# The norms of the two mixers: one full-precision product over all 512 squares, and a factor by logarithm and exponential

## The chip, the core and the metric

The kernel runs on one core of a Trainium2 chip. The metric is the device time of one execution in microseconds; below 1% of that time is a few of them, so small sums matter here. A core has TensorE (PE, with its weight loads shown apart as PEld), VectorE (DVE), ScalarE (ACT), GpSimd (POOL) and SyncE (SP), which issues nearly all DMAs. Each engine runs its own list of instructions in order and waits on semaphores.

## The reference, cut to what matters

One decoder block over 2048 tokens of 1024 features: an input projection, two mixers side by side (a gated linear recurrence with 4 heads of 128, and sliding-window attention with 8 heads of 64), an output projection over both, and a SwiGLU feed-forward network.

```python
# gated recurrence: each head is normed by itself, over its 128 features
o = o.transpose(0, 2, 3, 1, 4).reshape(bsz, s, A_HEADS, A_DV)
o = o * lax.rsqrt(jnp.mean(o * o, axis=-1, keepdims=True) + EPS)
o = o.reshape(bsz, s, A_WIDTH) * norm_g.astype(f32) * jax.nn.silu(g.astype(f32))
...
# attention: normed over all 512 features of its 8 heads
o = o.reshape(bsz, s, B_WIDTH)
return rmsnorm(o, norm_g).astype(q.dtype)
...
h = h + jnp.concatenate([y_a, y_b], axis=-1) @ w_out[l]
```

So per token there are five factors 1/sqrt(mean of squares + EPS): one for each of the four recurrence heads, one for the attention. They are what the change computes in another way.

## The kernel before, in words

The mixers run over four blocks of 512 tokens (`it` = 0 to 3). Features lie on the 128 partitions, the 512 tokens along the free dimension, so the sum of squares over features runs across partitions and is made by TensorE. Dense products split each operand in two parts of reduced precision, `hi` and `lo`, and run three products (lines 831 to 833); `whi`/`wlo`, `uhi`/`ulo` and `yhi`/`ylo` are such pairs. What is not split runs in full float32.

The order of all work is written out by hand. A block has slots 0 to 26. In slots 0 to 21 TensorE makes one group of 128 input columns (24 products of 512 tokens, `group`), and then the small steps of the mixers. In slots 22 to 26 it makes the first half of the output projection instead (`out_a`, by pieces k: 22 has k = 0 and 1; 23 has 2; 24 has 4 and 5; 25 has 6; 26 has 7 and 3), then `out_b` makes the other half. Piece k below 4 needs recurrence head k finished (`ylo`, L1809), piece k from 4 the attention's pair k - 4. Head a begins in slot 4, 9, 14 and 18; each later step has an offset from it. Every engine walks the same slots with its own code, and an instruction that waits holds up all that is behind it on its engine.

The norm of head a, in before:

- NORM_SUM, offset 6 (slots 10, 15, 20, 24). ScalarE has squared the head's output into `sqo`. TensorE runs `sums` (L847): four products with a 128x128 square block as weights and one column of `ones` moving, into bank X[3]. ScalarE takes the square root of 4 columns (L1264) into `hnrm`, VectorE the reciprocal (L1799) into `hrnrm`.
- NORM_MUL, offset 7 (slots 11, 16, 21, 25). TensorE runs `spread` (L838): four products of the factor's column, broadcast as weights, with the identity; this lays the factor of each token on all partitions of X[3]. VectorE multiplies `gate` by X[3] (L1805), ScalarE and VectorE split the result into `yhi` (L1268) and `ylo` (L1809).

The attention's norm does the same once a block, on bank X[1]: sum in slot 21 (root L1394, reciprocal L1861), spread in slot 22, then four multiplications (L1814), one for each pair.

Other names that the steps use: `make_hi` (L1201) and `make_lo` (L1663) split the weights of the unit two slots ahead, and can begin only when TensorE is through with the unit that lies in that buffer, that is with this slot's group; `cuminv` (L1752, VectorE) feeds `key` (L2243, GpSimd), which the product L970 of the next slot needs; `x_turn` number j (L1024; one a slot from slot 19 on) transposes a piece of x into X[0], and waits until ScalarE has copied number j - 1 out (`h`, L1307); `stats` (L1208, two in slot 24) and `roots` (L1214) prepare the norm of the next block's x, and VectorE scales that x after them (L1671, L1676). ScalarE holds one set of function tables at a time, and ACT_TABLE_LOAD changes it; Copy and Square need no change.

Of the kernel before, what the change touches and what calls it, by code (L numbers as in the profile page):

```python
# [36 lines left out]
ALU = mybir.AluOpType  # L37
ACT = mybir.ActivationFunctionType
AX_X = mybir.AxisListType.X

P = 128
# [89 lines left out]
def block_program(nc, x, ln1_g, w_in, lb_logits, hgrn_norm_g, attn_sinks, attn_norm_g, w_out, ln2_g,  # L131
# [37 lines left out]
    with ExitStack() as ctx:  # L169
# [80 lines left out]
        nrm = sb("nrm", [P, TB]); rnrm = sb("rnrm", [P, TB])  # L250
        hnrm = sb("hnrm", [P, TB]); hrnrm = sb("hrnrm", [P, TB])
        snrm = sb("snrm", [P, TB]); srnrm = sb("srnrm", [P, TB])
        mx = sb("mx", [P, 2]); nm = sb("nm", [P, 2, 2]); nms = sb("nms", [P, 2])
# [159 lines left out]
        s_srr = sem("s_srr")  # L413
        s_smul = sem("s_smul")
        s_yb = sem("s_yb")
# [31 lines left out]
        s_arr = sem("s_arr")  # L447
        s_amul = sem("s_amul")
        s_ya = sem("s_ya")
# [376 lines left out]
        def _(pe):  # L826
# [17 lines left out]
            def sums(bank, squares, done):  # L844

                for b in range(TB):
                    last = mm(bank[:, b:b + 1], squares[:, b * P:(b + 1) * P], ones[:, 0:1], start=True, stop=True)  # L847
                last.then_inc(done, 1)

# [102 lines left out]
            def iv_turn(it, a):  # L952
                pe.wait_ge(s_iv, it * HEADS + a + 1)
                if a:
                    pe.wait_ge(s_ya, it * HEADS + a)
                elif it:
                    pe.wait_ge(s_osb, it * TB)
                for b in range(TB):
                    last = tr(X[3][:, b * P:(b + 1) * P], ivT[:, b * P:(b + 1) * P], ident[:, :])
                last.then_inc(s_ivtr, 1)  # L960
# [49 lines left out]

            def head_mul(it, a):
                pe.wait_ge(s_arr, it * HEADS + a + 1)
                spread(X[3], hrnrm, s_amul)

# [33 lines left out]
            def slots(it):  # L1048

                for slot in range(SLOTS):  # L1050
                    if slot < IN_GROUPS and (it or slot >= 2):
                        group(it, slot)
                    for k in A_PLAN.get(slot, ()):
# [3 lines left out]
                        if k == A_PLAN[OUT_A][0]:  # L1057
                            key_turn(it, HEADS - 1)
                    a = head_at(slot, NORM_MUL)
                    if a is not None:  # L1060
                        head_mul(it, a)
                    a = head_at(slot, UPDATE)
# [4 lines left out]
                    if slot == SWA_SUM:  # L1067
                        pe.wait_ge(s_oacc, it * (PAIRS - 1) + PAIRS - 1)
                        sums(X[1], sqs[0], s_ssum)
                    if slot == SWA_MUL:  # L1070
                        pe.wait_ge(s_srr, it + 1)
                        spread(X[1], srnrm, s_smul)
                    for begin, step in ((SCORE, scores), (P_TURN, p_turn), (PV, pv)):
# [16 lines left out]
            def out_b(it):  # L1090
                for c, bank in zip(range(4, CS), (1, 2, 3, 0)):
                    n = OUT_B + c - 4
                    if bank == 1:
                        pe.wait_ge(s_yb, it * PAIRS + PAIRS)

# [96 lines left out]
        def _(act):  # L1192
# [61 lines left out]
            def output(it, a):  # L1254
                act.wait_ge(s_o, it * HEADS + a + 1)
                if a:
                    act.wait_ge(s_asum, it * HEADS + a)
                A(sqo[:, :], X[2][:, :], ACT.Square).then_inc(s_sq, 1)

            def head_sum(it, a):  # L1260
                act.wait_ge(s_asum, it * HEADS + a + 1)
                if a:
                    act.wait_ge(s_arr, it * HEADS + a)
                A(hnrm[:, :], X[3][:, 0:TB], ACT.Sqrt, scale=1.0 / P, bias=epst[:, 0:1]).then_inc(s_aroot, 1)  # L1264

# [87 lines left out]
            def slots(it):  # L1353
                for slot in range(SLOTS):
# [37 lines left out]
                    if slot == SWA_SUM:  # L1392
                        act.wait_ge(s_ssum, it + 1)
                        A(snrm[:, :], X[1][:, 0:TB], ACT.Sqrt, scale=1.0 / (PAIRS * P),  # L1394
                          bias=epst[:, 0:1]).then_inc(s_sroot, 1)
                    if slot == SWA_MUL:
# [237 lines left out]
        def _(dve):  # L1634
# [158 lines left out]

            def head_sum(it, a):
                n = it * HEADS + a
                dve.wait_ge(s_aroot, n + 1)
                if a:
                    dve.wait_ge(s_amul, n)
                V.reciprocal(hrnrm[:, :], hnrm[:, :]).then_inc(s_arr, 1)  # L1799

            def head_mul(it, a):
                n = it * HEADS + a
                dve.wait_ge(s_amul, n + 1)
                dve.wait_ge(s_y1, n + 1)
                V.tensor_tensor(gate[a % 2][:, :], gate[a % 2][:, :], X[3][:, :], ALU.mult).then_inc(s_ya, 1)  # L1805

# [5 lines left out]
            def swa_mul(it, p):  # L1812
                dve.wait_ge(s_osq, it * PAIRS + p + 1)
                V.scalar_tensor_tensor(out=oT[p][:, :], in0=oT[p][:, :], scalar=gb[:, p:p + 1],  # L1814
                                       in1=X[1][:, :], op0=ALU.mult, op1=ALU.mult).then_inc(s_yb, 1)

# [6 lines left out]
            def slots(it):  # L1823
                for slot in range(SLOTS):
# [32 lines left out]
                    if mul is not None:  # L1857
                        head_lo(it, mul)
                    if slot == SWA_SUM:
                        dve.wait_ge(s_sroot, it + 1)  # L1860
                        V.reciprocal(srnrm[:, :], snrm[:, :]).then_inc(s_srr, 1)  # L1861
                    if slot == SWA_MUL:
                        dve.wait_ge(s_smul, it + 1)
                        swa_mul(it, 0)
                    i = step_at(slot, PV)
                    if i is not None and i % TB == TB - 1:
                        dve.wait_ge(s_pv, it * STEPS + i + 1)
                        V.tensor_copy(oT[i // TB][:, :], M[3][:, :]).then_inc(s_oT, 1)
                    for offset, step in ((KEYS, keys), (UPDATE, update), (OUTPUT, output), (NORM_SUM, head_sum)):
                        a = head_at(slot, offset)  # L1870
# [472 lines left out]
```

## Time and profile before

| | us |
|---|---|
| before, median of 3 runs | 2281.8 |
| before, the 3 runs | 2279.1, 2281.8, 2285.85 |
| the profiled execution, its own time | 2285.81 |
| its span, first to last instruction | 2284.0 |
| TensorE busy in it | 2222.6 (97%) |
| VectorE busy | 1438.3 (63%) |
| ScalarE busy | 1010.2 (44%) |
| GpSimd busy | 443.8 (19%) |
| mean granted clock of TensorE | 0.992 |

The span is nearly the whole time. The four mixer blocks end about 958 us into the span, and the rest is the feed-forward network, which the change does not touch. TensorE's busy share is an upper figure, since its products are pipelined. The profile's chain of work that ended last is 86% TensorE.

### The profile page before, as it was taken

The page shows a single profiled execution, that of the slowest core. Times are in us where ns is not written, and L with a number is a line of the kernel's source. Part 1 is how long each engine was busy: PE and PEld are TensorE (multiplying, and loading weights), DVE is VectorE, ACT ScalarE, POOL GpSimd, SP SyncE. Part 2 cuts the span into 40 slices and gives each one's busy share as a digit, 9 for nine tenths or more (in the row PEclk, how much of TensorE's full clock was granted, in tenths as well). Part 3 has the DMA queues.
Part 4 walks back from the last instruction along what each step waited for, and adds up shares of the span by engine and source line. Part 5 has one row for each costly group of instructions (what it writes and reads, how often), then busy time and mean ns, then how long its engine had stood idle before and what let it go on. Part 6 is the DMA issues. An engine that isn't in the chain of part 4 may idle for free.

```text
span 2284.0 us, 29991 instructions
## 1 busy us (share of the span) xinstructions
PE 2222.6 (97%) x11144; PEld 1848.9 (81%) x11144; DVE 1438.3 (63%) x2170; ACT 1010.2 (44%) x1723; POOL 443.8 (19%) x344
## 2 busy tenths in 40 slices
PE   7999999999999999999999999999999999999997
PEld 6888878887888788878888887888788888887886
DVE  5775568656865677675566666467665555554555
ACT  5554455445554554444433333345533333333444
POOL 2231022201220122032233331000232222210000
PEclk9999999999999999999999999999999999999999
DMA  4222333233233313533345656788443232326765
GB/s 122 92 75 80 115 102 96 90 107 105 81 121 97 111 58 119 194 105 117 116 164 183 223 205 216 255 269 262 149 137 108 99 109 98 110 89 213 229 221 197
DMA packets 260705, 321.80 MB, mean 141 GB/s; under 512 B 17233, under 2 KB 168785, under 8 KB 259537
## 3 DMA queue, kind: packets, MB, share of 16 engines
q1 hardware_dynamic: 258256, 311.50, 41.5%
q10 hardware_dynamic: 2304, 8.39, 0.9%
q8 instruction: 89, 1.46, 0.3%
q14 instruction: 56, 0.45, 0.1%
HBM read 242.76 MB, written 77.07 MB: 140 GB/s over the span
## 4 chain that ended last, share of the span: by engine, by line
PE 86%; DVE 5%; issue 3%; ACT 3%; DMA 2%; POOL 0%; SPq 0%; ACTq 0%; DVEq 0%; POOLq 0%
PE M L1138 9%; PE M L1140 9%; PE M L1139 9%; PE M L831 7%; PE M L833 7%; PE M L832 7%; PE M L1165 3%; PE M L1167 3%; PE M L1166 3%; PE X L1165 3%; PE X L1166 3%; PE X L1167 3%; PE X L1140 3%; PE X L1139 3%; PE X L1138 3%
## 5 line engine op out<-in xcount | busy, mean ns | idle before, releaser
L2110 DVE TENSOR_TENSOR ring_lo<-ring_raw,ring_hi 128x1024 fp32r<-128x1024 f32 x154 | 189.4, 1230 | 186.9 <-ACT ring_hi L1566 186.5
L1663 DVE TENSOR_TENSOR wlo<-raw,whi 128x1024 fp32r<-128x1024 f32 x120 | 152.0, 1267 | 230.3 <-ACT whi L1201 230.1
L831 PE MATMUL M<-uhi,whi 128*128 128x512 f32 (+1 forms) x720 | 286.4, 398 | 3.7 <-DVE wlo L1663 2.1
L833 PE MATMUL M<-uhi,wlo 128*128 128x512 f32 (+1 forms) x720 | 278.7, 387 | 0.0
L832 PE MATMUL M<-ulo,whi 128*128 128x512 f32 (+1 forms) x720 | 278.1, 386 | 0.0
L1566 ACT ACTIVATE ring_hi<-ring_raw 128x1024 fp32r<-128x1024 f32 x154 | 162.8, 1059 | 239.4 <-DMA ring_raw<-a_scr 236.2
L1138 PE MATMUL M<-t_hi,wu_hi 128*128 128x512 f32 x616 | 240.8, 391 | 4.1 <-DVE gq L2032 2.3
L1140 PE MATMUL M<-t_hi,wu_lo 128*128 128x512 f32 x616 | 240.6, 391 | 0.0
L1139 PE MATMUL M<-t_lo,wu_hi 128*128 128x512 f32 x616 | 240.4, 390 | 0.0
L1201 ACT ACTIVATE whi<-raw 128x1024 fp32r<-128x1024 f32 x120 | 126.6, 1055 | 196.9 <-PE M L833 146.2
L2000 DVE TENSOR_TENSOR wu_lo<-fraw,wu_hi 128x512 fp32r<-128x512 f32 x132 | 127.5, 974 | 120.3 <-ACT wu_hi L1507 120.0
L2254 POOL TENSOR_TENSOR pr<-pr,rd 128x512 f32<-128x512 f32 x64 | 84.4, 1318 | 539.7 <-DVE rd L1696 539.7
L831 PEld LDWEIGHTS M<-uhi,whi 128*128 128x128 f32 x720 | 136.9, 190 | 32.3 <-issue 4.2
L833 PEld LDWEIGHTS M<-uhi,wlo 128*128 128x128 f32 x720 | 136.4, 189 | 27.9
L2306 POOL TENSOR_TENSOR fs<-fraw 128x512 f32<-128x512 f32 x44 | 64.8, 1474 | 481.1 <-DMA fraw<-in_w_gate_dram 214.9
L832 PEld LDWEIGHTS M<-ulo,whi 128*128 128x128 f32 x720 | 137.1, 190 | 24.3
L1138 PEld LDWEIGHTS M<-t_hi,wu_hi 128*128 128x128 f32 x616 | 115.9, 188 | 29.8 <-DVE wu_lo L2000 5.6
L1165 PE MATMUL M<-ring_hi 128*128 128x512 f32 x308 | 123.1, 400 | 15.4 <-DVE ring_lo L2110 15.4
L1139 PEld LDWEIGHTS M<-t_lo,wu_hi 128*128 128x128 f32 x616 | 116.1, 188 | 24.1
L1140 PEld LDWEIGHTS M<-t_hi,wu_lo 128*128 128x128 f32 x616 | 116.0, 188 | 24.1
L2312 POOL TENSOR_TENSOR fraw<-fraw,fs 128x512 f32<-128x512 f32 x44 | 57.4, 1305 | 372.1 <-DVE wl_lo L2000 372.0
L1277 ACT ACTIVATE pr<-pr,nm 128x256 f32<-128x256 f32 x128 | 64.2, 502 | 145.0 <-DVE nms L1722 145.0
(277 smaller groups left out, 5109.3 us busy)
## 6 DMA issues: line engine op xcount, KB each, us to landing
raw<-in_w_in_dram SPq DMA_DIRECT2D x88, 512.0 KB, 3.8
ring_raw<-a_scr SPq DMA_DIRECT2D x154, 256.0 KB, 3.6
fraw<-in_w_gate_dram SPq DMA_DIRECT2D x44, 512.0 KB, 4.6
fraw<-in_w_up_dram SPq DMA_DIRECT2D x44, 512.0 KB, 4.8
a_scr<-au SPq DMA_DIRECT2D x88, 256.0 KB, 2.3
ring_raw<-t_scr SPq DMA_DIRECT2D x88, 256.0 KB, 3.0
a_scr<-gq SPq DMA_DIRECT2D x66, 256.0 KB, 2.5
ring_raw<-in_w_down_dram SPq DMA_DIRECT2D x66, 256.0 KB, 3.0
```

The lines of the kernel that those rows point to most:

```text
L831: mm(bank, whi[s][:, kb, :], hi, start=first, stop=False)
L832: mm(bank, whi[s][:, kb, :], lo, start=False, stop=False)
L833: return mm(bank, wlo[s][:, kb, :], hi, start=False, stop=last)
L1138: mm(bank[:, :], wh[:, k, :], hi[:, k, :], start=start and k == 0, stop=False, skip_group_check=True)
L1139: mm(bank[:, :], wh[:, k, :], lo[:, k, :], start=False, stop=False, skip_group_check=True)
L1140: last = mm(bank[:, :], wl[:, k, :], hi[:, k, :], start=False, stop=k == KH - 1, skip_group_check=True)
L1165: mm(banks[b][:, :], hi[:, 1, tokens], hi[:, 0, :], start=first, stop=False, skip_group_check=True)
L1166: mm(banks[b][:, :], hi[:, 1, tokens], lo[:, 0, :], start=False, stop=False, skip_group_check=True)
L1167: done = mm(banks[b][:, :], lo[:, 1, tokens], hi[:, 0, :], start=False, stop=last, skip_group_check=True)
L1566: A(hi[:, :, :], raw_r[:, :, :], ACT.Copy).then_inc(s_rowhi, 1)
L1663: V.tensor_tensor(wlo[s][:, :, :], raw[s][:, :, :], whi[s][:, :, :].bitcast(F32), ALU.subtract).then_inc(s_lo[s], 1)
L2110: V.tensor_tensor(lo[:, :, :], raw_r[:, :, :], hi[:, :, :].bitcast(F32), ALU.subtract).then_inc(s_rowlo, 1)
```

## The change

The sum becomes one full-precision product for all 512 tokens: weights `ones` (128x128), moving operand the 512 columns of squares. As all 128 rows of the weights are ones, each token's sum arrives on all partitions at once, and `spread` is not needed for these two norms (it stays for the norm behind the output projection). ScalarE makes the factor for 128x512 values: exp(-0.5 * ln(mean + EPS)), with Ln from the bank into `sqo` (attention: `sqs[0]`, in the trace `gu`) and Exp in place there. VectorE multiplies by that tile and no longer by a bank of PSUM; both reciprocals are gone.

```diff
             def sums(bank, squares, done):
 
-                for b in range(TB):
-                    last = mm(bank[:, b:b + 1], squares[:, b * P:(b + 1) * P], ones[:, 0:1], start=True, stop=True)
-                last.then_inc(done, 1)
+                mm(bank[:, :], ones[:, :], squares[:, :], start=True, stop=True).then_inc(done, 1)
...
             def iv_turn(it, a):
                 pe.wait_ge(s_iv, it * HEADS + a + 1)
                 if a:
-                    pe.wait_ge(s_ya, it * HEADS + a)
+                    pe.wait_ge(s_aroot, it * HEADS + a)
...
-            def head_mul(it, a):
-                pe.wait_ge(s_arr, it * HEADS + a + 1)
-                spread(X[3], hrnrm, s_amul)
...
-                    if slot == SWA_MUL:
-                        pe.wait_ge(s_srr, it + 1)
-                        spread(X[1], srnrm, s_smul)
...
                     if bank == 1:
-                        pe.wait_ge(s_yb, it * PAIRS + PAIRS)
+                        pe.wait_ge(s_sroot, it + 1)
...
             def head_sum(it, a):
                 act.wait_ge(s_asum, it * HEADS + a + 1)
-                if a:
-                    act.wait_ge(s_arr, it * HEADS + a)
-                A(hnrm[:, :], X[3][:, 0:TB], ACT.Sqrt, scale=1.0 / P, bias=epst[:, 0:1]).then_inc(s_aroot, 1)
+                A(sqo[:, :], X[3][:, :], ACT.Ln, scale=1.0 / P, bias=epst[:, 0:1]).then_inc(s_aroot, 1)
+                act.wait_ge(s_aroot, it * HEADS + a + 1)
+                A(sqo[:, :], sqo[:, :], ACT.Exp, scale=-0.5).then_inc(s_arr, 1)
...
                         act.wait_ge(s_ssum, it + 1)
-                        A(snrm[:, :], X[1][:, 0:TB], ACT.Sqrt, scale=1.0 / (PAIRS * P),
-                          bias=epst[:, 0:1]).then_inc(s_sroot, 1)
+                        A(sqs[0][:, :], X[1][:, :], ACT.Ln, scale=1.0 / (PAIRS * P), bias=epst[:, 0:1]).then_inc(s_sroot, 1)
+                        act.wait_ge(s_sroot, it + 1)
+                        A(sqs[0][:, :], sqs[0][:, :], ACT.Exp, scale=-0.5).then_inc(s_srr, 1)
...
-                V.reciprocal(hrnrm[:, :], hnrm[:, :]).then_inc(s_arr, 1)
...
-                dve.wait_ge(s_amul, n + 1)
+                dve.wait_ge(s_arr, n + 1)
                 dve.wait_ge(s_y1, n + 1)
-                V.tensor_tensor(gate[a % 2][:, :], gate[a % 2][:, :], X[3][:, :], ALU.mult).then_inc(s_ya, 1)
+                V.tensor_tensor(gate[a % 2][:, :], gate[a % 2][:, :], sqo[:, :], ALU.mult).then_inc(s_ya, 1)
...
                 V.scalar_tensor_tensor(out=oT[p][:, :], in0=oT[p][:, :], scalar=gb[:, p:p + 1],
-                                       in1=X[1][:, :], op0=ALU.mult, op1=ALU.mult).then_inc(s_yb, 1)
+                                       in1=sqs[0][:, :], op0=ALU.mult, op1=ALU.mult).then_inc(s_yb, 1)
```

How the lists of instructions change is seen at three places. The first is ScalarE in block 0 from the end of slot 20, where head 2 is summed, into slot 21, where the attention is (`gu` is the attention's sum, `whi` the weights of unit 23, `gate` the gate of head 3, `kst` its keys). Before:

```order
L1264 ACT_TABLE_LOAD [waits s_arr]
L1264 ACTIVATE hnrm<-X,epst 128x4 [waits s_asum]
L1307 ACTIVATE h<-X 128x4x128 [waits s_xtr]
L1201 ACTIVATE whi_56<-raw_54 128x1024 [waits s_raw1,s_group]
L1240 ACT_TABLE_LOAD [waits s_yalo]
L1240 ACTIVATE gate_114<-M 128x512 [waits s_group]
L1268 ACTIVATE yhi<-gate_113 128x512 [waits s_ya]
L1394 ACT_TABLE_LOAD
L1394 ACTIVATE snrm<-X,epst 128x4 [waits s_ssum]
L1246 ACTIVATE iv<-X 128x512 [waits s_o,s_ivtr]
L1307 ACTIVATE h<-X 128x4x128 [waits s_xtr]
L1252 ACTIVATE kst<-X 128x512 [waits s_upd,s_ktr]
```

Now:

```order
L1252 ACT_TABLE_LOAD
L1252 ACTIVATE sqo<-X,epst 128x512 [waits s_asum]
L1254 ACT_TABLE_LOAD
L1254 ACTIVATE sqo<-sqo 128x512 [waits s_aroot]
L1297 ACTIVATE h<-X 128x4x128 [waits s_xtr]
L1191 ACTIVATE whi_56<-raw_54 128x1024 [waits s_raw1,s_group]
L1230 ACTIVATE gate_110<-M 128x512 [waits s_yalo,s_group]
L1258 ACTIVATE yhi<-gate_109 128x512 [waits s_ya]
L1384 ACT_TABLE_LOAD
L1384 ACTIVATE gu_63<-X,epst 128x512 [waits s_ssum]
L1386 ACT_TABLE_LOAD
L1386 ACTIVATE gu_63<-gu_63 128x512 [waits s_sroot]
```

The square root of head 2 has become table load, Ln, table load, Exp ahead of `h` and `whi`; the load that stood ahead of `gate` is gone; the attention's root has become the same four, and `iv`, `h` and `kst` follow them.

The second is ScalarE in slots 24 and 25 of block 0, head 3's norm, with the statistics of the next block's x behind it. Before:

```order
L1264 ACTIVATE hnrm<-X,epst 128x4 [waits s_arr,s_asum]
L1208 ACTIVATE pr_dump,xss<-os_69 128x1024 [waits s_x0_0]
L1208 ACTIVATE pr_dump,xss<-os_70 128x1024 [waits s_xss,s_x0_1]
L1214 ACTIVATE xnrm<-xss,epst 128x2 [waits s_xn,s_xss]
L1307 ACTIVATE h<-X 128x4x128 [waits s_xtr]
L1201 ACTIVATE whi_55<-raw_53 128x1024 [waits s_raw0,s_group]
L1268 ACTIVATE yhi<-gate_114 128x512 [waits s_ya]
```

Now:

```order
L1252 ACT_TABLE_LOAD
L1252 ACTIVATE sqo<-X,epst 128x512 [waits s_asum]
L1254 ACT_TABLE_LOAD
L1254 ACTIVATE sqo<-sqo 128x512 [waits s_aroot]
L1198 ACTIVATE pr_dump,xss<-os_69 128x1024 [waits s_x0_0]
L1198 ACTIVATE pr_dump,xss<-os_70 128x1024 [waits s_xss,s_x0_1]
L1204 ACT_TABLE_LOAD [waits s_xn]
L1204 ACTIVATE xnrm<-xss,epst 128x2 [waits s_xss]
L1297 ACTIVATE h<-X 128x4x128 [waits s_xtr]
L1191 ACTIVATE whi_55<-raw_53 128x1024 [waits s_raw0,s_group]
L1258 ACTIVATE yhi<-gate_110 128x512 [waits s_ya]
```

Ahead of the two `pr_dump` now stand a load, Ln, a load and Exp where one short root stood, and the root of x (`xnrm`) has a load of its own, since Exp has taken the place of the square root's tables. The copy `h` and `yhi` stand behind all of it. In all, the program has 62 table loads, and had 47.

The third is TensorE in slot 21 of block 0, behind the slot's group: the spread of head 2, the attention's sum, and the small products of head 3. Before:

```order
L838 MATMUL X<-ident,hrnrm 128x128 [waits s_arr]
L838 MATMUL X<-ident,hrnrm 128x128 x3
L847 MATMUL X<-ones,gu_63 128x1 [waits s_oacc]
L847 MATMUL X<-ones,gu_63 128x1 x3
L970 MATMUL X<-qdec_112,key 128x128 [waits s_y1,s_qdec,s_key]
L970 MATMUL X<-qdec_112,key 128x128 x3
L959 MATMUL X<-ident,ivT 128x128 [waits s_ya,s_iv]
L959 MATMUL X<-ident,ivT 128x128 x3
L1024 MATMUL X<-ident,xs_72 128x128 [waits s_xT,s_xh2]
L1024 MATMUL X<-ident,xs_72 128x128 x3
```

Now:

```order
L845 MATMUL X<-gu_63,ones 128x512 [waits s_oacc]
L967 MATMUL X<-qdec_108,key 128x128 [waits s_y1,s_qdec,s_key]
L967 MATMUL X<-qdec_108,key 128x128 x3
L956 MATMUL X<-ident,ivT 128x128 [waits s_aroot,s_iv]
L956 MATMUL X<-ident,ivT 128x128 x3
L1019 MATMUL X<-ident,xs_72 128x128 [waits s_xT,s_xh2]
L1019 MATMUL X<-ident,xs_72 128x128 x3
```

The four spreading products are gone, the four sums are one product, and the transposition of `ivT` waits for the logarithm of head 2 (s_aroot) and no longer for its multiplication (s_ya).

## Rows read from the trace of the kernel before

**Rows 1.** The page: span, and TensorE in its part 1.

```profile
span 2284.0 us, 29991 instructions
...
PE 2222.6 (97%) x11144; PEld 1848.9 (81%) x11144; DVE 1438.3 (63%) x2170; ACT 1010.2 (44%) x1723; POOL 443.8 (19%) x344
```

**Rows 2.** Lines, ScalarE: line, operation, tiles, count | busy us, mean ns | idle before.

```profile
L1277 ACT ACTIVATE pr<-pr,nm 128x256 f32<-128x256 f32 x128 | 64.2, 502 | 145.0 <-DVE nms L1722 145.0
...
L1307 ACT ACTIVATE h<-X 128x512 f32<-128x512 f32 x32 | 18.8, 589 | 19.1 <-PE X L1024 19.1
...
L1264 ACT ACT_TABLE_LOAD x12 | 15.4, 1283 | 0.2
...
L1300 ACT ACTIVATE yhi<-oT 128x512 fp32r<-128x512 f32 x16 | 10.1, 631 | 20.6 <-DVE oT L1814 20.4
```

**Rows 3.** Timeline, block 0, slots 10 to 11: start us, duration us, what [idle before].

```profile
101.07 1.05 PE L847 MATMUL X<-ones,sqo 128*128 128x1 f32 x8
...
101.98 0.48 PE L831 MATMUL M<-uhi,whi 128*128 128x512 f32 x1
...
105.06 1.28 ACT L1264 ACT_TABLE_LOAD   x1
...
107.51 1.05 PE L838 MATMUL X<-ident,hrnrm 128*128 128x128 f32 x8
...
108.32 0.71 PE L923 MATMUL X<-kk,qs 128*128 128x256 f32 x4
```

**Rows 4.** Timeline, head 1, slots 11 to 12 of block 0.

```profile
114.01 1.54 POOL L2243 TENSOR_TENSOR key<-key,cuminv 128x512 f32<-128x512 f32 x1 [4.81 <-DVE cuminv L1752]
...
117.18 1.16 PE L970 MATMUL X<-qdec,key 128*128 128x128 f32 x8
```

**Rows 5.** Timeline, head 1, slots 11 to 12 of block 1.

```profile
356.87 1.55 POOL L2243 TENSOR_TENSOR key<-key,cuminv 128x512 f32<-128x512 f32 x1 [4.67 <-DVE cuminv L1752]
...
359.51 1.16 PE L970 MATMUL X<-qdec,key 128*128 128x128 f32 x8
```

**Rows 6.** Timeline, block 0, slots 20 to 23.

```profile
190.76 1.28 ACT L1264 ACT_TABLE_LOAD   x1
...
192.22 0.59 ACT L1307 ACTIVATE h<-X 128x512 f32<-128x512 f32 x1
...
193.04 1.06 ACT L1201 ACTIVATE whi<-raw 128x1024 fp32r<-128x1024 f32 x1 [0.22 <-PE M L833]
...
196.04 0.69 DVE L1755 SCALAR_TENSOR_TENSOR gate<-gate,M 128x512 f32<-128x512 f32 x1 [0.28 <-ACT gate L1240]
...
196.31 0.48 PE L831 MATMUL M<-yhi,whi 128*128 128x512 f32 x1
...
202.36 1.05 PE L838 MATMUL X<-ident,srnrm 128*128 128x128 f32 x8
...
208.21 1.16 PE L994 MATMUL X<-amask,iv 128*128 128x128 f32 x8 [0.37 <-DVE st L1782]
```

**Rows 7.** Timeline, block 0, slots 24 to 26.

```profile
216.87 0.95 PE L847 MATMUL X<-ones,sqo 128*128 128x1 f32 x8
...
217.85 0.26 ACT L1264 ACTIVATE hnrm<-X,epst 128x4 f32<-128x4 f32 x1 [2.45 <-PE X L847]
...
220.43 0.29 ACT L1214 ACTIVATE xnrm<-xss,epst 128x2 f32<-128x2 f32 x1
...
220.63 0.58 ACT L1307 ACTIVATE h<-X 128x512 f32<-128x512 f32 x1
...
221.80 0.60 PE L1024 MATMUL X<-ident,xs 128*128 128x128 f32 x4
...
225.82 0.50 PE L831 MATMUL M<-yhi,whi 128*128 128x512 f32 x1 [0.67 <-DVE ylo L1809]
```

**Rows 8.** Timeline, block 3, slots 24 to 25.

```profile
946.98 0.59 ACT L1307 ACTIVATE h<-X 128x512 f32<-128x512 f32 x1
...
948.97 0.60 PE L1024 MATMUL X<-ident,xs 128*128 128x128 f32 x4
```

More of the change, by code:

```diff
@@ L250, in block_program @@
         nrm = sb("nrm", [P, TB]); rnrm = sb("rnrm", [P, TB])
-        hnrm = sb("hnrm", [P, TB]); hrnrm = sb("hrnrm", [P, TB])
-        snrm = sb("snrm", [P, TB]); srnrm = sb("srnrm", [P, TB])
         mx = sb("mx", [P, 2]); nm = sb("nm", [P, 2, 2]); nms = sb("nms", [P, 2])
@@ L413, in block_program @@
         s_srr = sem("s_srr")
-        s_smul = sem("s_smul")
         s_yb = sem("s_yb")
@@ L447, in block_program @@
         s_arr = sem("s_arr")
-        s_amul = sem("s_amul")
         s_ya = sem("s_ya")
@@ L1058, in slots @@
                             key_turn(it, HEADS - 1)
-                    a = head_at(slot, NORM_MUL)
-                    if a is not None:
-                        head_mul(it, a)
                     a = head_at(slot, UPDATE)
@@ L1256, in output @@
                 if a:
-                    act.wait_ge(s_asum, it * HEADS + a)
+                    act.wait_ge(s_ya, it * HEADS + a)
                 A(sqo[:, :], X[2][:, :], ACT.Square).then_inc(s_sq, 1)
@@ L1792, in output @@
                                        in1=gate[a % 2][:, :], op0=ALU.mult, op1=ALU.mult).then_inc(s_y1, 1)
[L1794 to L1798, printed above, removed]
-                V.reciprocal(hrnrm[:, :], hnrm[:, :]).then_inc(s_arr, 1)
             def head_mul(it, a):
                 n = it * HEADS + a
-                dve.wait_ge(s_amul, n + 1)
+                dve.wait_ge(s_arr, n + 1)
                 dve.wait_ge(s_y1, n + 1)
-                V.tensor_tensor(gate[a % 2][:, :], gate[a % 2][:, :], X[3][:, :], ALU.mult).then_inc(s_ya, 1)
+                V.tensor_tensor(gate[a % 2][:, :], gate[a % 2][:, :], sqo[:, :], ALU.mult).then_inc(s_ya, 1)
             def head_lo(it, a):
@@ L1858, in slots @@
                         head_lo(it, mul)
-                    if slot == SWA_SUM:
-                        dve.wait_ge(s_sroot, it + 1)
-                        V.reciprocal(srnrm[:, :], snrm[:, :]).then_inc(s_srr, 1)
                     if slot == SWA_MUL:
-                        dve.wait_ge(s_smul, it + 1)
+                        dve.wait_ge(s_srr, it + 1)
                         swa_mul(it, 0)
@@ L1868, in slots @@
                         V.tensor_copy(oT[i // TB][:, :], M[3][:, :]).then_inc(s_oT, 1)
-                    for offset, step in ((KEYS, keys), (UPDATE, update), (OUTPUT, output), (NORM_SUM, head_sum)):
+                    for offset, step in ((KEYS, keys), (UPDATE, update), (OUTPUT, output)):
                         a = head_at(slot, offset)
```

## The prediction, made before the changed kernel ran

> **What bounds the kernel now.** I read the page first. TensorE is busy 2222.6 of 2284.0 us [rows 1], so an instruction taken off its list is worth its time, but only if nothing else becomes late. The timeline of a quiet place, slots 10 and 11 of block 0, shows the price of the norm there [rows 3]: the sums stand from 101.07 to 101.98 (0.91 us), the spread from 107.51 to 108.32 (0.81 us), and TensorE waits for neither. That the spread needs no wait shows that root and reciprocal are hidden behind the group of slot 11 (24 products in 5.53 us, 0.230 us each). Then I looked for places where the reserve of the other engines is small, by the timelines at the ends of the change: head 1's keys [rows 4, 5], the attention's norm [rows 6], head 3's norm [rows 7, 8]. There TensorE already waits a little: 0.37 us for VectorE's `st` [rows 6] and 0.67 us for `ylo` [rows 7]. In these slots ScalarE works off a queue, and a thing put into that queue is late for everybody behind it.
>
> **TensorE's list.** There are 20 norms (4 blocks, 4 heads and one attention). Each loses 0.91 us of sums and 0.81 us of spread [rows 3]; at 202.36 only the spread goes with it. Each gains one float32 product of 512 columns, a form that the trace does not have. Lower bound: a float32 product leaves two records, and if each takes a column as fast as the split products do, it is 2 x 0.230 = 0.46 us [rows 3]. Upper bound: the four products at 117.18 also move 512 float32 columns in all, and last to about 118.17 (1.16 us less some 0.17 of overlap), 0.99 us [rows 4]. I take 0.90, near the row with the same columns. So the list becomes shorter by 0.91 + 0.81 - 0.90 = 0.82 us for a norm, 16.4 us in all (0.73 to 1.26 each, 15 to 25 us). This is what could be gained if nothing else moved.
>
> The Trainium skill (FP8 and Floating Point Precision, TensorE Precision Notes) says that true float32 takes four passes through the array. Four passes at the rate of rows 3 would be 0.92 us, and the list would then be shorter by 0.80 us for a norm; no row here shows the passes themselves.
>
> **ScalarE's list.** The root was a load of 1.28 us and 0.26 us of work. Now it is load, Ln, load, Exp. Loads take 1.283 us [rows 2]. Ln reads 512 columns from PSUM with a pointer as bias: the PSUM copy of that shape takes 0.589 [rows 2]. What a pointer bias adds: 631 ns for 512 columns [rows 2] and 1.06 us for 1024 [rows 6] give 0.84 ns a column, so 256 columns are 0.42, and the Exp with bias of that size takes 0.502 [rows 2], 0.09 more. Ln is 0.68. Exp in SBUF is 0.63, as L1300. With 0.02 between two: 1.28 + 0.68 + 1.30 + 0.64 = 3.90, was 1.55. So everything behind a norm stands about 2.35 us later, and up to 1.3 of that is given back where a load for Exp or Tanh follows (it is gone now). Over the kernel ScalarE gets some 20 x 1.05 us and 15 loads more, about 40 us on an engine busy 44%; the amount is hidden, the places count.
>
> The same skill (ScalarE: Activation LUTs, Table sets) says that ln and then exp need one load only, since one set has both. The compiled list of the changed kernel contradicts it, with a load between the two; the row's 1.283 us is what the page gives for the load itself. If the rule held, each norm would stand 1.3 us less late. The sum below would be -6.6 in the quiet places, -3.3 in slots 20 to 23, +7.2 for head 3 and 0 in block 3, in all -2.7 us.
>
> **Slots 10 to 12 and 15 to 17 (heads 0 and 1), 8 places.** After the load at 105.06 [rows 3] Exp ends at 105.06 + 3.90 = 108.96, and only then the weights of unit 13 are split, which before began at about 107.7, 0.2 behind the group. They are 1.25 us late; VectorE's multiplication no longer waits for the spread, so `make_lo` and with it `cuminv` come 0.9 us late in block 0. In block 1 the multiplication and the weights' `lo` ran later on VectorE than the group alone asks for, so I count 0.4 there. `key` ends at 115.55 and is wanted at 117.18: 1.63 us of reserve [rows 4]. In block 1 it is 358.42 against 359.51, 1.09 [rows 5]. So 0.7 us of reserve is left in both, less than the 0.82 that TensorE saves: it arrives early and waits for `key`. I take a gain of 0.65 a place, 8 x 0.65 = 5.2 us. Bounds: 1.26 x 8 = 10, and 0.2 x 8 = 1.6 if the delay is 0.9 in all places (1.09 - 0.9).
>
> **Slots 20 to 23 (head 2 and the attention), 4 places.** ScalarE begins its load at 190.76 [rows 6], when it is free; nothing that TensorE saves moves that. Then `h`, which was at 192.22, begins at 190.76 + 3.92 = 194.68 and ends at 195.27. TensorE's transposition number 2 waits for it, and slot 22 begins at 195.7 instead of 196.31. `whi` begins at 195.3 and not 193.04, lasts 1.06, its `lo` on VectorE 1.23, and behind it stands the gate of head 3, from 197.65 instead of 196.04, done at 198.3. The third bank of slot 22 is the one that this gate reads: TensorE wants it after six products, at 195.7 + 1.4 = 197.1, and waits until 198.35; before it got there at 197.7. So slot 22's group ends 0.65 us later (203.0, was 202.36). ScalarE meanwhile has `yhi`, load, Ln, load, Exp, `iv`, `h`, `kst`: from 196.95, 0.6 + 3.9 + 0.6 + 0.6 + 0.6, to 203.2. So `kst` and the weights of unit 24 come at the same late time. VectorE's `st` follows these weights, 0.7 us later, and TensorE's output product at 208.21 waits for it already. The spread's 0.97 at 202.36 is gone, but the wait grows by it. Loss 0.7 us a place, 2.8 us. Bounds: 0 (the gate is not late) and 1.0.
>
> **Slots 24 to 26 (head 3), blocks 0 to 2.** Here ScalarE is idle until the sum is there, so its first load is hidden. The sum starts at 216.87 [rows 7]; the root started at 217.85. With the new product, Ln starts between 217.5 and 218.0. Ahead of the statistics of x stand then 0.68 + 1.30 + 0.64 = 2.62 us and not 0.16, and ahead of their root one more load, 1.30. So `xnrm`, at 220.43 before, starts at 220.43 + 2.46 + 1.30 = 224.2, give or take 0.25, and `h` ends at 225.0 and not 221.21. TensorE's next transposition (221.80 before) waits for that `h`: 3.3 us later. VectorE walks the same way: it scales x first, and then multiplies head 3, so `ylo` comes 3.75 us later, and the product that waited at 225.82 [rows 7] starts at 229.6. It waited before, so nothing is hidden: 3.7 us a block, 11.1 for three. Bounds 3.4 and 4.0. The piece of x for the last transposition is ordered behind these weights and shifts along.
>
> **Block 3** has no statistics; ScalarE splits one operand there, as before. `h` was at 946.98 and ended at 947.57; with 2.46 more it ends at 950.0, TensorE wanted it at 948.97 [rows 8]. Loss about 1.1 us, between 0.9 and 1.4.
>
> **The sum:** -5.2 + 2.8 + 11.1 + 1.1 = +9.8 us on the profiled execution's 2285.81 us, 2295.6. The medians are 4 us lower: 2281.8 + 9.8 = 2291.6 us. The terms' bounds add to between -10 + 0 + 10.2 + 0.9 = +1 and -1.6 + 4 + 12 + 1.4 = +16, so this case alone gives 2283 to 2298; runs of one kernel spread by some 3 us around their median.
>
> **The rivals.**
>
> A. TensorE's shorter list shows in full: all 20 places give 0.82 us, 16.4 us in all, time 2265.4 (to 2257 with the cheap product). For it: 97% busy, and the profile names hardly any wait of TensorE. Against it: the two waits above exist at just the places where ScalarE's queue grows, and the order puts `h` behind four instructions more. This is faster than before. 7%.
>
> B. The keys do not hold TensorE in slots 12 and 17, and slots 20 to 23 lose nothing, so only head 3 counts: 8 x 0.82 = 6.6 gained, 12.2 lost, and the attention's places even: +5.6, 2287.4. For it: GpSimd's durations are rough, and the key's reserve is the smallest number of this working. It is no change that can be measured (within 0.3%, 6.8 us, is what I call the same). 21%.
>
> C. The product is dear: each of its records takes the 512 columns at half the rate of the four small products, 1.8 us. Then the saving is gone in the 8 quiet places, Ln starts 0.9 us later in slot 24, and 0.9 more is lost in slot 21: 9.8 + 5.2 + 3.6 + 3.6 = +22, 2304. Against it: rows 4 move as many float32 columns in 0.99 us. 7%.
>
> D. The change removes more than it says or the sums wait elsewhere: a reserve opens somewhere in `out_b` or at the entry of the feed-forward part that takes back half of head 3's delay, +4, 2286. Against it: no wait stands in `out_b` before. 5%.
>
> **How the numbers follow.** The forecast has 60%: slower by 9.8 us, of which about a tenth of its own width falls below 6.8. Slower by over 0.3%: 54 of it, C's 7 and a little of B: 0.62. The same: most of B, D, and the low end of the forecast (6): 0.30. Faster: A and a trace of the rest, 0.08. The range leaves out A and the upper end of C: 2281 to 2299.
>
> **What would show it right or wrong.** In the profile after, TensorE should wait for ScalarE's `h` at the transposition of slot 25 by about 4 us in blocks 0 to 2, and for VectorE's `ylo` behind it by about 1; for the gate (in slot 22) by about 1.2 us; its wait for `st` in slot 23 should be near 1.4 us and not 0.37; and its wait for `key` should appear in slots 12 and 17. Idle time of TensorE in the mixers should be up by about 26 us, its list shorter by 16. Ln should show as 0.68 us, the product as 0.90 between its start and the next one. I am wrong if TensorE arrives at slot 25's transposition later than `h`, or if the product differs from 0.46 to 0.99 us.

## The result, and the profile after

The changed kernel takes 2303.9 us (median of 4 runs, 2301.9 to 2305.0), the kernel before in the same comparison 2283.2 us (4 runs): ratio 1.0088, with a 95% interval of 1.0073 to 1.0103. That is 20.7 us slower, where 9.8 were forecast. The profiled execution took 2303.22 us, 17.4 more than that of before; before's lay 2.6 us above its own median.

The page of the changed kernel, the rows that answer to [rows 1]:

```profile
span 2301.6 us, 29422 instructions
...
PE 2213.6 (96%) x10864; PEld 1823.1 (79%) x10864; DVE 1435.2 (62%) x2150; ACT 1047.1 (45%) x1758; POOL 442.6 (19%) x344
```

TensorE's list is 9.0 us shorter by its busy time, where 16 were forecast (products at half clock, below, lengthen it again), and the span is 17.6 us longer, so TensorE is idle 26.6 us more. ScalarE is busy 37 us more; about 40 was forecast. Now its groups by line (operation, tiles, count | busy us, mean ns | idle before), beside [rows 2]:

```profile
L1252 ACT ACT_TABLE_LOAD x16 | 20.5, 1283 | 0.3
L1254 ACT ACT_TABLE_LOAD x16 | 20.5, 1283 | 0.3
...
L1252 ACT ACTIVATE sqo<-X,epst 128x512 f32<-128x512 f32 x16 | 11.0, 689 | 5.0 <-PE X L845 4.9
...
L1254 ACT ACTIVATE sqo<-sqo 128x512 f32<-128x512 f32 x16 | 10.1, 631 | 0.2
```

Ln takes 689 ns and Exp 631, as worked out beforehand (0.68, 0.63), and a table load stands ahead of each: 16 ahead of Ln and 16 ahead of Exp in the heads alone. The Trainium skill (ScalarE: Activation LUTs, Table sets) says that ln and exp share a table set and need one load; these rows contradict it, and the 1283 ns of a load are what the same page gives.

What TensorE waited for, after the change: line <- releaser: us in total, times, longest us.

```profile
PE X L1019 <- ACT h L1297: 14.0, 4, 4.0
...
PE X L967 <- POOL key L2224: 8.2, 6, 2.4
PE X L975 <- ACT iv L1236: 7.8, 4, 2.0
PE X L991 <- DVE st L1773: 5.0, 4, 1.3
PE M L943 <- DVE oT L1849: 2.7, 4, 0.8
...
PE X L1019 <- DMA xs<-in_x_dram: 1.7, 3, 0.6
...
PE M L830 <- DVE gate L1746: 1.6, 4, 0.4
PE X L845 <- POOL gu L2274: 1.5, 4, 0.4
```

The same view of the kernel before:

```profile
PE X L970 <- POOL key L2243: 7.2, 3, 2.4
PE X L1024 <- DMA xs<-in_x_dram: 3.3, 3, 1.2
...
PE M L831 <- DVE ylo L1809: 2.0, 3, 0.7
...
PE X L994 <- DVE st L1782: 1.5, 4, 0.4
```

Reading the two against each other is most of the answer. `h`, 14.0 us in 4 waits, is the wait that was forecast at slot 25 (4.0 us in each of the first three blocks, 1.9 in block 3). `st` grew from 0.37 to 1.24 us a block, near the 1.4 forecast. The gate is waited for 0.4 us a block, where 1.2 was forecast, and the wait for `ylo` of about 1 us that was to follow `h` is not there. But `iv` with 7.8 us is new, and the prediction does not have it. `oT` with 2.7 us is not in it either, nor are the four waits of 0.4 us for `gu`, the attention's squares from GpSimd.

**Where the time went.** I took the start of each TensorE instruction that both kernels have, after minus before, and read how this offset changes in each stretch of the program. Signs: plus is later.

```
stretch                     block 0  block 1  block 2  block 3     sum  forecast
entry of the kernel                                              -0.84         -
slots 0 to 20 (heads 0, 1)    -1.46    -0.56    -0.27    -0.42   -2.7       -5.2
slots 20 to 23                +2.84    +4.41    +2.84    +4.42  +14.5       +2.8
slots 24 to 26                +3.37    +3.42    +3.41     0.0   +10.2      +12.2
feed-forward part                                                -3.7         0
```

With 0.2 us between the blocks this makes 17.7 us, the span's difference. Block 3 loses 1.2 us at slot 25, as forecast, and gets it back before the feed-forward part begins, so its entry in the table is 0. The large miss is the third line.

The change does not touch the part of the last line; there the two profiled executions differ in the clock. The one of before ran its feed-forward part at half clock for 20.5 us, that of after for 13.7 us (both without the last microseconds of the program). One stretch of before that has no partner after the change moves the offset by 1.6 of the 3.7 us (window of the kernel before: length, busy us of the engines, then the granted clock as a share of 2.4 GHz, DMA share, GB/s):

```profile
999.75:1003.15 3.40, 3.40 (x10) 2.63 (x9) 0.64 (x2) 0.00 (x0) 1.28 (x1) 0.50 0.85 291
```

Where the feed-forward part begins, the changed kernel is 21.4 us behind.

**Slots 20 to 23, block 0.** The timeline after (start us, duration us, what [idle before]), for [rows 6]:

```profile
190.01 0.69 ACT L1252 ACTIVATE sqo<-X,epst 128x512 f32<-128x512 f32 x1
...
192.01 0.63 ACT L1254 ACTIVATE sqo<-sqo 128x512 f32<-128x512 f32 x1
...
192.55 0.58 ACT L1297 ACTIVATE h<-X 128x512 f32<-128x512 f32 x1
...
193.02 1.05 ACT L1191 ACTIVATE whi<-raw 128x1024 fp32r<-128x1024 f32 x1
...
193.97 0.59 ACT L1230 ACTIVATE gate<-M 128x512 f32<-128x512 f32 x1
...
195.10 1.28 ACT L1384 ACT_TABLE_LOAD   x1
...
196.06 0.51 PE L830 MATMUL M<-yhi,whi 128*128 128x512 f32 x1 [0.40 <-DVE gate L1746]
...
196.39 0.69 ACT L1384 ACTIVATE gu<-X,epst 128x512 f32<-128x512 f32 x1
...
198.39 0.63 ACT L1386 ACTIVATE gu<-gu 128x512 f32<-128x512 f32 x1
198.93 0.58 ACT L1236 ACTIVATE iv<-X 128x512 f32<-128x512 f32 x1
...
199.65 0.63 PE L975 MATMUL X<-ident,forget 128*128 128x128 f32 x4 [1.96 <-ACT iv L1236]
...
208.75 1.16 PE L991 MATMUL X<-amask,iv 128*128 128x128 f32 x8 [1.24 <-DVE st L1773]
```

And one more row of the kernel before, the same transposition of `forget`:

```profile
199.15 0.60 PE L978 MATMUL X<-ident,forget 128*128 128x128 f32 x4
```

The order is the one forecast: load, Ln, load, Exp, then `h` at 192.55, `whi` at 193.02, the gate at 193.97. But all of it is about 2 us earlier than forecast (192.55 and not 194.68), since ScalarE came to the head's load with TensorE's own gain, which the prediction had excluded. So the gate costs only 0.40 us. Then comes the attention's own load, Ln, load, Exp from 195.10 to 199.02, and only behind them the copy of `iv` out of bank X[3]. The transposition at 199.65 writes into this bank and has to wait 1.96 us for the copy. Before, it stood at 199.15 and waited for nothing. In offsets: +0.57 for the gate, +2.23 at `iv`, -0.85 for the spread that is gone, +0.89 for `st` at 208.75: +2.84.

**Slots 24 to 26, block 0,** for [rows 7]:

```profile
218.47 0.69 ACT L1252 ACTIVATE sqo<-X,epst 128x512 f32<-128x512 f32 x1 [1.23 <-PE X L845]
...
220.47 0.63 ACT L1254 ACTIVATE sqo<-sqo 128x512 f32<-128x512 f32 x1
...
224.69 0.29 ACT L1204 ACTIVATE xnrm<-xss,epst 128x2 f32<-128x2 f32 x1
224.90 0.58 ACT L1297 ACTIVATE h<-X 128x512 f32<-128x512 f32 x1
...
225.62 0.63 PE L1019 MATMUL X<-ident,xs 128*128 128x128 f32 x4 [4.01 <-ACT h L1297]
```

`xnrm` at 224.69 (forecast 224.2), `h` from 224.90 to 225.48 (225.0), the transposition at 225.62 after a wait of 4.01 us (about 4). This step was right.

**The clock.** The granted clock of four windows, two in the kernel after (same view as above):

```profile
226.30:229.70 3.40, 3.40 (x10) 2.68 (x9) 3.40 (x5) 1.24 (x3) 0.00 (x0) 0.54 0.02 5
448.20:451.60 3.40, 3.40 (x11) 2.67 (x10) 0.00 (x0) 0.60 (x1) 0.00 (x0) 0.53 0.00 0
```

and in the kernel before, first a stretch of its own and then the place in the program that 448.20 is in the kernel after:

```profile
313.70:317.10 3.40, 3.16 (x14) 3.07 (x15) 2.37 (x4) 3.26 (x4) 3.22 (x3) 0.50 0.04 7
441.50:444.90 3.40, 3.40 (x19) 2.88 (x18) 0.00 (x0) 0.62 (x2) 0.00 (x0) 1.00 0.03 11
```

In the first three TensorE runs at its lower level of 1.2 GHz (0.54 and 0.53 because those windows begin a little ahead of the stretch): a split product takes 0.43 us there and not 0.23. After the change the mixers have 8 such stretches of some 3.4 us (27.3 us), before it they had 3 (10.2 us). Three of the eight stand at the places of before, at about 320, 568 and 817 us; there TensorE waits 2.4 us for `key` in both kernels. The other five begin within 1.2 us after the start of an instruction that had waited for `h` or `iv`. All three `h` waits of 4.0 us are followed by one, and of the four `iv` waits of 1.9 to 2.0 us those at 447.69 and in block 3. A stretch costs up to 1.6 us. In blocks 1 and 3 that is paid in full in slots 22 and 23 (4.41 and 4.42 against 2.84). In slots 25 and 26 it is absorbed by waits that stood there anyway, for `ylo` and for x.

**The quiet places.** In block 0 the offset falls by 0.76 us where the spread stood, in slot 11 and again in slot 16, close to the 0.82 forecast, and 0.33 is given back in slot 17. In the later blocks more is given back: TensorE waits 0.23 to 0.58 us for `key` in slot 12, and in slot 17 there is this, after the change (timeline as above):

```profile
404.96 0.68 DVE L1849 COPY oT<-M 128x512 f32<-128x512 f32 x1
...
405.78 0.66 PE L943 MATMUL M<-pT,vals 128*64 128x128 f32 x8 [0.79 <-DVE oT L1849]
```

The same two before the change:

```profile
399.98 0.68 DVE L1868 COPY oT<-M 128x512 f32<-128x512 f32 x1
...
402.12 0.66 PE L946 MATMUL M<-pT,vals 128*64 128x128 f32 x8
```

There the copy ended 1.46 us ahead of the product. Now the product waits 0.79 us for it, about all that head 1's norm had saved. VectorE works without a pause up to the copy: the head's multiplication, which waits for the Exp, then the weights' `lo`, the attention's step, `cuminv` and `ylo`.

### The profile page after: what moved, and what is told of

The parts are those of the page before. It is cut to its first block, busy times and chain, and to the rows that moved or that the text cites. A ratio compares the mean times of both kernels' runs of the same rounds, so it can differ in the third digit from the quotient of the medians.

```text
span 2301.6 us, 29422 instructions
## 1 busy us (share of the span) xinstructions
PE 2213.6 (96%) x10864; PEld 1823.1 (79%) x10864; DVE 1435.2 (62%) x2150; ACT 1047.1 (45%) x1758; POOL 442.6 (19%) x344
## 3 DMA queue, kind: packets, MB, share of 16 engines
q10 hardware_dynamic: 2304, 8.39, 0.9%
## 4 chain that ended last, share of the span: by engine, by line
PE 77%; DVE 8%; ACT 7%; issue 6%; DMA 2%; POOL 1%; SPq 0%; ACTq 0%; DVEq 0%; POOLq 0%
PE M L1128 9%; PE M L1130 9%; PE M L1129 9%; PE M L830 5%; PE M L832 5%; PE M L831 5%; PE M L1155 3%; PE M L1156 3%; PE M L1157 3%; PE X L1155 3%; PE X L1156 3%; PE X L1157 3%; PE X L1130 3%; PE X L1128 3%; PE X L1129 3%
```

## The experiments

All times are medians; a ratio is to the kernel before in the same comparison, with its 95% interval. The kernel before measured 2282.7 to 2283.6 us in them.

**1. The heads' norms only.** The change for the 16 norms of the recurrence heads; the attention's norm stays four sums, root, reciprocal and spread.

```diff
-  sums(X[1], sqs[0], s_ssum)              # one product of 512 columns
+  sums_old(X[1], sqs[0], s_ssum)          # four products of one column
-  A(sqs[0], X[1], ACT.Ln, ...); A(sqs[0], sqs[0], ACT.Exp, scale=-0.5)
+  A(snrm, X[1][:, 0:TB], ACT.Sqrt, ...)   # and reciprocal, spread(X[1], srnrm)
```

> Only the four recurrence heads are normed the new way; the attention keeps four sums, square root, reciprocal and spread. Theory Q (ScalarE's queue ahead of iv): the attention's load, Ln, load, Exp stand ahead of iv, on which TensorE's transposition of kstate waits, and cost 2.8 us a block and 1.6 more in two blocks where the clock fell; without them the kernel is some 12 to 15 us faster than the full change: about 2290, +7 us on before, of which 10 are the three blocks of head 3 in slot 25. Rival H (the heads' own queue does it, by head 2's norm at the end of slot 20): only the 0.8 us of the attention's own work changes and the time stays near 2300.

**2. The attention's norm only,** the mirror image: heads as before the change, attention as after it.

```diff
-  A(sqo, X[3], ACT.Ln, ...); A(sqo, sqo, ACT.Exp, scale=-0.5)
+  A(hnrm, X[3][:, 0:TB], ACT.Sqrt, ...)   # and reciprocal, spread(X[3], hrnrm)
```

> Only the attention is normed the new way; the heads as before. Theory Q: the load, Ln, load, Exp of the attention still stand ahead of iv, but they start about 2.3 us earlier than with head 2's new norm in front, so iv is late by some 1 us at most: +1 to +6 us on before, 2284 to 2289. Its wait shows as TensorE waiting for iv. Rival H: no wait for iv at all, and one spread less: 0 to -3 us, 2280 to 2283.

Measured: heads only 2290.0 us, 1.0030 [1.0018, 1.0041]; attention only 2286.8, 1.0011 [1.0002, 1.0021]. With the heads only the wait for `iv` is gone and `st` is back at 1.4 us in all, while `h` stays at 14.0. With the attention only, `iv` costs 7.4 us of waiting and `st` 4.9, against 7.8 and 5.0 in the whole. The time lies in the range expected, but `iv` was to be late by 1 us at most. In block 0 of this kernel:

```profile
198.79 0.63 ACT L1398 ACTIVATE gu<-gu 128x512 f32<-128x512 f32 x1
199.33 0.58 ACT L1248 ACTIVATE iv<-X 128x512 f32<-128x512 f32 x1
...
200.05 0.63 PE L982 MATMUL X<-ident,forget 128*128 128x128 f32 x4 [1.84 <-ACT iv L1248]
```

So the attention's four instructions make TensorE wait for `iv` by themselves; head 2's new norm ahead of them is not needed for it.

The parts cost 6.4 and 3.3 us, together 9.7, where the whole costs 20.7. The waits do not tell why, since each part has nearly those that it has in the whole. The granted clock accounts for the larger part. The four profiled executions, in us at half clock (feed-forward part without the last microseconds of the program):

```
kernel            mixers  feed-forward part  clock, median of its runs
before              10.2               20.5                      0.9940
heads only          17.1               10.2                      0.9920
attention only       6.8               10.2                      0.9955
full change         27.3               13.7                      0.9905
```

Against before, the whole has 10.3 us more at half clock, and the parts have 3.4 and 13.7 us less. The last column gives an estimate over all runs: the distance of the clock to 1, times the kernel's time, is 13.7, 18.3, 10.3 and 21.9 us, so the clock costs the whole 8.2 us more than before and the two parts together 1.2 us more. That is some 7 of the 11 us by which the parts fall short of the whole. It differs between runs of one kernel too, in before from 0.991 to 0.996, and no run sets it apart, so this stays an estimate.

**3. `iv` copied before the attention's logarithm.** One instruction of ScalarE's list moved from slot 22 to slot 21.

```diff
   if slot == SWA_SUM:
+      iv_turn(it, HEADS - 1)
       act.wait_ge(s_ssum, it + 1)         # then Ln and Exp of the attention
...
-  if a is not None:
+  if a is not None and not (slot == SWA_SUM and step is iv_turn):
```

> The full change, but in slot 21 ScalarE copies iv before the attention's logarithm. Theory Q: TensorE's wait for iv (1.96 us in four blocks) is gone, and with it the fall of the clock behind it; what is left there is the wait for kst and the weights' chain, 0.7 us a block as first forecast: 2.1 x 4 + 1.6 x 2 = 11.6 us faster than the full change, about 2292. Rival K (the wait only moves: kst stands behind the same chain, and the product L984 waits for it as long): within 2 us of the full change's 2304.

**4. Statistics and root of the next block's x one slot earlier,** in slot 23 and not 24, so that head 3's four instructions don't stand ahead of them.

```diff
-  if slot == X_STATS:                     # stats, roots of x_next
+  if slot == X_STATS - 1 and it + 1 < NSB:
```

> The full change, but ScalarE takes the statistics and the root of the next block's x in slot 23 (idle there), one slot earlier, so that nothing of x stands between head 3's Exp and the copy h. My term for head 3: TensorE's wait of 4.0 us for h in three blocks shrinks to under 0.5 and the wait for ylo with it: 3.4 x 3 = 10 us faster than the full change, about 2294. Rival (the x root's table load and the shifted work only land on another wait in slot 24): within 3 us of 2304.

**5. Both.**

> The full change with both moves: iv ahead of the attention's logarithm, and the statistics and root of the next x in slot 23. If the two delays are separate terms they add: 2303.9 - 12.7 - 10.2 = 2281, at or 2 us under before. Rival (they share the time, since what is taken off slots 20 to 23 is waited for in slot 25 by a DMA or by kst): 2286 to 2290.

Measured: `iv` first 2291.2 us, 1.0036 [1.0023, 1.0048]; statistics early 2293.7, 1.0041 [1.0026, 1.0055]; both 2280.9, 0.9987 [0.9979, 0.9996]. TensorE's waits with `iv` first:

```profile
PE X L1019 <- ACT h L1297: 14.0, 4, 4.0
...
PE X L991 <- DVE st L1774: 5.0, 4, 1.3
```

and with the statistics early:

```profile
PE X L975 <- ACT iv L1236: 7.8, 4, 2.0
PE X L1019 <- DMA xs<-in_x_dram: 7.3, 4, 2.4
...
PE X L1019 <- ACT h L1297: 1.9, 1, 1.9
```

The three times are within 1 us of those expected. Each edit takes away one wait and leaves the other. `iv` first brings 12.7 us: some 2.0 a block in the offsets of slots 20 to 23 (about 0.8 is left, near the 0.7 forecast), and 3.1 for the two stretches of low clock in blocks 1 and 3. The remaining 1.6 are spread. The statistics bring 10.2 us and uncover a wait of up to 2.4 us for the DMA of x, which `h` had hidden. The `h` wait that is left is the one of block 3, which has no statistics of x. Together they bring 23.0 us, the sum of the two (22.9). This settles both places.

**6. Heads 0 and 1 only.** These are the quiet places by themselves.

```diff
-  sums(X[3], sqo, s_asum)
+  if a < 2: mm(X[3], ones, sqo, ...)      # one product; Ln, Exp behind it
+  else:     sums(X[3], sqo, s_asum)       # four; root, reciprocal, spread
```

> Only heads 0 and 1, whose norms fall in slots 10 and 15, are normed the new way; heads 2 and 3 and the attention as before. This is my term for the quiet places alone, forecast at 8 x 0.65 = 5.2 us; the trace of the full change says 2.7. Now: 2.7 us faster than before, about 2281. Rival (the saving is real in full, 8 x 0.82, and only the late slots spoil it): 6.5 us faster, 2277.

Measured: 2280.1 us, 0.9982 [0.9973, 0.9992], 3.5 us faster than before. So the half of TensorE's saving that the offsets show is real, and the other half goes into `key` (7.9 us, 6 waits; before 7.2, 3) and `oT` (2.7, 4 waits; before none).

**7. The heads' norms, with the statistics early** (the edits of 1 and 4).

> The heads the new way, the attention as before, and the statistics of the next x in slot 23. Heads alone were +6.4 us on before, of which 10 are head 3's in slot 25: so 2290 - 10 = 2280, 3 us faster than before, if the terms add. Rival (they do not): above 2284.

Measured: 2274.6 us, 0.9959 [0.9946, 0.9971]. This is 5.5 us better than expected. The expectation took experiment 1 and subtracted 10 us for head 3's place. Against experiment 1, TensorE waits 1.9 us for `h` in place of 14.0 and 4.6 for the DMA of x in place of 2.0, 9.5 us less, and the mixers ran at half clock for 3.4 us in place of 17.1, four stretches fewer, at 1.57 us each up to 6.3 us. Together that is at most 15.8; the medians lie 15.4 apart. Against before, two stretches fewer are up to 3.1 of the 9.1 us, and they followed waits of 2.4 us for `key` that both kernels have.

**8. No table loads for the factor.** Ln and Exp are made Square: same shapes, no load.

```diff
-  A(sqo, X[3], ACT.Ln, scale=1.0 / P, bias=epst)
+  A(sqo, X[3], ACT.Square, scale=1.0 / P, bias=epst)
-  A(sqo, sqo, ACT.Exp, scale=-0.5)
+  A(sqo, sqo, ACT.Square, scale=-0.5)
```

> Full change, but Ln and Exp are replaced by Square with the same operands and sizes, which no table load precedes: the factor is not computed, and the program has 22 loads instead of 62. This tells the loads from the work. If the loads make the lateness (2 x 1.3 of the 2.35 to 3.9 us in each norm): TensorE's waits for iv and h fall to nearly nothing and some 20 to 24 us come back, 2280 to 2284, or under before. If the 512-column functions and the places in the queue do: over half of the 20 us stays, above 2292.

This kernel does not compute the factor. Measured: 2280.3 us, 0.9982 [0.9973, 0.9991], 23.6 us faster than the full change with the same instructions otherwise. TensorE's waits:

```profile
PE X L1019 <- ACT h L1297: 8.9, 4, 2.7
PE X L967 <- POOL key L2224: 7.2, 3, 2.4
PE X L991 <- DVE st L1773: 4.9, 4, 1.2
PE X L845 <- POOL gu L2274: 3.5, 4, 0.9
```

No wait for `iv` is left, `h` is down from 14.0 to 8.9, `key` is back at three waits, as before. The mixers have 3 stretches at half clock in place of 8. The loads, 62 after the change and 22 here, are what makes ScalarE late. Functions of the size of Ln and Exp could be borne. That the time is 3.3 us below before does not price the product alone, since before has 47 loads.

**9. The attention's logarithm behind the weights of slot 22,** with the statistics early, and VectorE's product of it behind its other work of that slot.

```diff
-  if slot == SWA_SUM:                     # ScalarE: Ln and Exp of the attention
+  if slot == SWA_MUL:
...
-  if slot == SWA_MUL: swa_mul(it, 0)      # VectorE, ahead of the heads' steps
+  # the same, behind them
```

> The full change with the statistics early, and the attention's load, Ln, load, Exp in slot 22 behind the split of that slot's weights; VectorE's first product of the attention behind the state updates. Neither iv, kst nor the weights then stand behind the attention's chain, and TensorE's wait for st (1.2 us) goes as well: 1 us a block less than heads only with early statistics (2274.6), about 2270. Rival: the first pair's ylo is now late for slot 24, a new wait of 1 to 3 us a block: 2276 to 2284.

Measured: 2289.7 us, 1.0029 [1.0018, 1.0041], worse than either theory. The rows of its waits that bear on it:

```profile
PE X L1019 <- DMA xs<-in_x_dram: 12.9, 3, 4.3
...
PE X L991 <- DVE st L1771: 2.3, 4, 0.6
```

`iv` and `st` were cured (`st` 2.3 us in all), but TensorE now waits for the DMA of x, 12.9 us in three waits. The attention's work ends later in slot 22 and 23, the statistics of x behind it, and the buffer whose transfer feeds the last transpositions comes free later. That this is the chain was not tried apart; the wait is measured, its cause on that queue is my reading.

**10. Exp of heads 0 and 1 behind the weights,** on top of experiment 7, with VectorE's `make_lo` ahead of its multiplication there, so that the weights are not late.

```diff
+  def head_exp(it, a): ...                # the Exp alone
   # ScalarE, slots 11 and 16: make_hi, then
+  if a is not None and a < 2: head_exp(it, a)
   # VectorE: make_lo, then
+  if mul is not None and mul < 2: head_mul(it, mul)
```

> Heads the new way, attention as before, statistics early (2274.6), and for heads 0 and 1 ScalarE's Exp behind the split of the weights, VectorE's split ahead of the multiplication. If the late weights are what holds key and oT in slots 12 and 17 (the step that made my gain of 5.2 us into 2.7), they come about 0.9 us earlier and up to 0.8 us a place in 6 to 8 places comes back: 2270. Rival (VectorE's whole list holds them, whatever comes first): within 1.5 us of 2274.6.

Measured: 2273.7 us (2273.3 to 2274.6), 0.9960 [0.9946, 0.9973]. Within 0.9 us of experiment 7, whose interval overlaps it: no gain shown. `key` still waits 8.1 us in 7 waits, `oT` 2.8 in 4. So the weights were not what held the key. `cuminv` stands on VectorE behind the multiplication either way; that this holds it is read from the list and was not tried apart. This and experiment 7 are the best versions, some 9 us faster than the kernel before.

## Why the prediction was wrong

- **Direction and mechanism.** Slower, through ScalarE's queue at the two places named: right. The size was off by a factor of two, and the time fell outside the range.
- **Slots 20 to 23: the step that failed.** It was the sentence "Loss 0.7 us a place, 2.8 us. Bounds: 0 (the gate is not late) and 1.0." The prediction listed ScalarE's queue rightly, "`yhi`, load, Ln, load, Exp, `iv`, `h`, `kst`", but asked only for the gate, `kst` and the weights who waits for it. It did not ask it of `iv`. Its own numbers end `iv` at 196.95 + 0.6 + 3.9 + 0.6, near 202, while TensorE comes to the transposition that overwrites the bank of `iv` at 199.15 or, with its gain, earlier. A second sentence fell with it: "nothing that TensorE saves moves that", of ScalarE's load at 190.76. It moved to 188.71. Instead of 0.7 us a block it was 2.84, and 4.4 where a stretch of low clock followed. Experiment 2 has the same wait, 1.84 us a block, with the attention's norm alone. Experiment 3 moves that copy alone and gives 12.7 us back, and lands 0.4 us from the time forecast for the whole change, some of it by errors of the other terms that cancel.
- **The clock.** The prediction has no term for it. Five more stretches came in the mixers, two of them paid in slots 22 and 23: 3.1 us. The feed-forward part, put at 0, shows -3.7 us between the two profiled executions, of which at least 1.6 and up to 3.1 come from before's two further stretches at half clock there; where that part begins, the offset is 21.4 us.
- **The quiet places** gave 2.7 us and not 5.2. `key` came as the prediction said, but 0.2 to 0.6 us of wait stood in slot 12, and the wait for `oT` in slot 17 was not seen: the reserve of that copy was never read. Experiment 6 measures the places at 3.5 us.
- **Slots 24 to 26** were right in size: 3.4 us a block against 3.7 (the wait for `ylo` behind `h` did not show), 10.2 with block 3 against 12.2. Block 3 lost 1.2 at the place (1.1 forecast), but gave it back behind it.
- **TensorE's product** fits 0.90. It starts at 191.37, and the next instruction starts 0.96 us later; in slot 10 sum and start of the group took 0.05 us less than the four sums. **Ln, Exp, loads**: 689, 631 and 1283 ns, as taken.
- **Rivals.** A, the list's saving in full, was far off. C gives 2304, the time that was measured, for a reason that did not occur: the product is not dear. Its time is a coincidence. B was half right, in that the keys held TensorE little in slot 12; but slots 20 to 23 lost the most of all.

## What to carry to other kernels

When an instruction is put into a queue, walk down everything that stands behind it and ask of each who waits for it; a copy that empties a buffer has a waiter too, the one who writes the buffer next. Count table loads as part of a formula's price: logarithm and exponential by turns cost 2.6 us of loads each time here, more than the arithmetic (1.3 us), and the same list without the loads was 23.6 us faster. Look at the granted clock of both executions before adding up parts: here two parts of a change cost 9.7 us and the whole 20.7, with nearly the same waits. A change that does not pay as a whole can pay in the places where its queue has room: the heads' norms with the statistics moved out of their way gave 9 us, the attention's norm took 6 of them back even with its copy of `iv` moved (experiments 5 and 7).

## What the runs showed of the hardware

Waits of TensorE within a dense stream were followed by stretches of half clock (1.2 GHz). The long ones always were: the three waits of 4.0 us for `h` in the full change and in experiments 1 and 3, and the three of 4.3 us for the DMA of x in experiment 9, 12 of 12; the clock fell between 0.8 us before TensorE went on and 1.2 us after. Each kernel here, before too, has three waits of 2.4 us for `key` in the mixers, and of these 36 waits 23 were; all three in before and in the full change, one of three in experiments 7 and 10. Of the five waits of 1.9 to 2.0 us in the full change two were, of the four of 1.84 us in experiment 2 none. Each such stretch lasted about 3.4 us (one, in experiment 1, 6.8) and cost 1.57 us where no later wait took it up. I had counted a wait at its own length only. What decides between the waits that are followed and those that are not stays open.
